# Gated heads in tiles of 128 tokens: three states a head instead of seven, and the output product, norm and rounding one block sooner

## The reference

```python
b = jnp.cumsum(chunks(log_a, dk), axis=2)
b_last = b[:, :, -1:]
q_dec = q * jnp.exp(b)
k_intra = k * jnp.exp(-b)
k_state = k * jnp.exp(b_last - b)

causal = jnp.tril(jnp.ones((C, C), dtype=bool))
scores = jnp.einsum('bnchk,bnshk->bnhcs', q_dec, k_intra)
scores = jnp.where(causal, scores, 0.0)
o_intra = jnp.einsum('bnhcs,bnshv->bnchv', scores, v)

def step(state, inp):
    q_c, k_c, v_c, decay = inp
    o_c = jnp.einsum('bchk,bhkv->bchv', q_c, state)
    state = state * jnp.exp(decay)[..., None] + jnp.einsum('bchk,bchv->bhkv', k_c, v_c)
    return state, o_c
...
o = rmsnorm(o, norm_g).reshape(B, T, D_MODEL)
o = o * jax.nn.silu((r + b_r).astype(f32))
return o.astype(h.dtype) @ w_o
```

## Time and profile before

| | |
|---|---|
| median of 3 runs | 1520.91 us (1520.56 to 1521.14) |
| span of the profiled execution | 1519.9 us |
| TensorE (PE) busy | 1500.9 us, 99% of the span |
| DVE, ACT, POOL busy | 991.4, 658.3, 172.3 us |
| DMA | 182.04 MB, mean 120 GB/s |

### The profile page before, as it was taken

One profiled execution on the slowest core, in us unless ns is written; L12 is line 12 of the kernel. 1 busy time (PEld: TensorE's weight loads), 2 busy tenths in 40 slices (PEclk: granted clock), 3 DMA queues, 4 the chain that ended last, 5 costly groups with the idle time before them and its releaser, 6 DMA issues.

```text
span 1519.9 us, 18779 instructions
## 1 busy us (share of the span) xinstructions
PE 1500.9 (99%) x7424; PEld 1231.2 (81%) x7424; DVE 991.4 (65%) x1620; ACT 658.3 (43%) x1125; POOL 172.3 (11%) x180
## 2 busy tenths in 40 slices
PE   9999999999999999999999999999999999999998
PEld 7788878888888888877777978888888976778786
DVE  7677667966666664877776743434344549989774
ACT  4554444513233233555565532413233446556660
POOL 0000001000000002111111100000000103676200
PEclk9999999999999999999999999999999999999999
DMA  9435444566656653122212343333333231212131
GB/s 374 143 113 166 140 138 149 186 215 183 202 186 201 185 160 107 47 79 70 70 56 84 97 123 92 98 100 94 100 95 99 76 96 61 70 56 72 41 111 56
DMA packets 52840, 182.04 MB, mean 120 GB/s; under 512 B 5984, under 2 KB 7008, under 8 KB 52752
## 3 DMA queue, kind: packets, MB, share of 16 engines
q1 hardware_dynamic: 52752, 180.83, 37.8%
HBM read 177.27 MB, written 3.41 MB: 119 GB/s over the span
## 4 chain that ended last, share of the span: by engine, by line
PE 89%; DVE 6%; ACT 2%; POOL 2%; issue 1%; DVEq 0%; ACTq 0%
PE PS L544 23%; PE PS L547 23%; PE PS L545 23%; PE PS L610 2%; PE PS L824 1%; PE PS L843 1%; PE PS L557 1%; PE PS L554 1%; PE PS L555 1%; POOL sb_TMD L2536 1%; PE PS L1134 1%; PE PS L1140 1%; PE PS L1135 1%; PE PS L629 1%; DVE sb_Wl L1780 1%
## 5 line engine op out<-in xcount | busy, mean ns | idle before, releaser
L544 PE MATMUL PS<-sb_Hh,sb_Wh 128*128 128x512 f32 x1000 | 399.4, 399 | 0.2 <-ACT sb_rg L1376 0.2
L547 PE MATMUL PS<-sb_Hh,sb_Wl 128*128 128x512 f32 x1000 | 390.9, 391 | 0.6 <-DVE sb_Wl L1780 0.6
L545 PE MATMUL PS<-sb_Hl,sb_Wh 128*128 128x512 f32 x1000 | 390.6, 391 | 0.0
L1187 ACT ACTIVATE sb_Wh<-sb_RAW 128x1024 fp32r<-128x1024 f32 x217 | 228.2, 1052 | 287.4 <-PE PS L547 280.7
L1780 DVE TENSOR_TENSOR sb_Wl<-sb_RAW,sb_Wh 128x1024 fp32r<-128x1024 f32 x217 | 268.5, 1238 | 69.6 <-ACT sb_Wh L1187 69.6
L544 PE MATMUL PS<-sb_Oh,sb_Wh 128*128 128x512 f32 x600 | 235.2, 392 | 0.4 <-ACT sb_rg L1376 0.4
L547 PE MATMUL PS<-sb_Oh,sb_Wl 128*128 128x512 f32 x600 | 233.7, 389 | 0.0
L545 PE MATMUL PS<-sb_Ol,sb_Wh 128*128 128x512 f32 x600 | 233.5, 389 | 0.0
L544 PEld LDWEIGHTS PS<-sb_Hh,sb_Wh 128*128 128x128 f32 x1000 | 188.1, 188 | 52.1 <-issue 13.2
L547 PEld LDWEIGHTS PS<-sb_Hh,sb_Wl 128*128 128x128 f32 x1000 | 188.0, 188 | 41.7 <-DVE sb_Wl L1780 1.3
L545 PEld LDWEIGHTS PS<-sb_Hl,sb_Wh 128*128 128x128 f32 x1000 | 188.2, 188 | 39.1 <-issue 1.2
(11 more groups left out here) (433 smaller groups left out, 2061.4 us busy)
## 6 DMA issues: line engine op xcount, KB each, us to landing
sb_RAW<-w SPq DMA_DIRECT2D x128, 512.0 KB, 3.6
sb_ARW<-ada SPq DMA_DIRECT2D x86, 512.0 KB, 4.4
sb_RAW<-diff_in SPq DMA_DIRECT2D x24, 512.0 KB, 3.6
sb_RAW<-gla_in SPq DMA_DIRECT2D x20, 512.0 KB, 3.7
sb_RAW<-in_b SPq DMA_DIRECT2D x16, 512.0 KB, 3.8
sb_RAW<-gla_wo SPq DMA_DIRECT2D x8, 512.0 KB, 3.7
sb_RAW<-diff_wo SPq DMA_DIRECT2D x8, 512.0 KB, 3.5
sb_RAW<-wo SPq DMA_DIRECT2D x8, 512.0 KB, 3.6
```

The source lines that it names most:

```text
L544: mm(to[0:m, :], WH[si][:, k, 0:m], hi[:, k, :], start=first, stop=False)
L545: mm(to[0:m, :], WH[si][:, k, 0:m], lo[:, k, :], start=False, stop=False)
L547: ins = mm(to[0:m, :], WL[si][:, k, 0:m], hi[:, k, :], start=False, stop=last)
L1187: act(WH[slot_of(b)][:, :, 0:m], RAWS[raw_of(b)][:, 0:8 * m].rearrange("p (k m) -> p k m", k=8), ACT.Copy).then_inc(*done("w_hi", b))
```

## The change

Scores, states and outputs are worked out in four tiles of 128 tokens (two chunks) instead of eight chunks, with three states between them.

- **Scores.** The mask `tri` becomes causal over 128 tokens. The key side of `ki` holds only for the same chunk, so `gla_scores` adds, behind the four products of a head, four more of 64x64 that overwrite the corner "second chunk's queries with first chunk's keys", from the new buffer `KS` (decayed keys; its slot 0 is the first chunk of a tile, slot 2 the second, slot 1 the first one times the second's decay, for the state).
- **States.** `KS` takes the place of the buffer `kst` in the ring TD. DVE adds one product of 128x192 into slot 1 (signal `g_ks2`) and a tile's decay `tdec` of 128x4; transposes go from four to three; the increments are three products of all 128 rows and 256 columns; the recurrence has three instructions.
- **Output.** DVE adds one product of 128x192 that gives the first state's decay to the second chunk's queries (third slot of `qd`, signal `g_qo`). `gla_out` has one product of 128 columns with a state for each tile but the first, whose operand is slots 0 and 2 of `qd`.
- **Steps.** "head" has three steps: 1 scores and all states, 2 output, 3 norm and rounding. Head 0 has them at ticks 9 to 11, head 1 at 11 to 13, head 2 at 17 to 19, head 3 at 23 to 25. "r" stands before "head" in the table, and DVE no longer sorts its list.

```diff
-    GLA_TASKS += [(_first[3], "head", _h, 4)] + ([(_first[4], "gates", _h + 1, 1)] if 0 < _h < 3 else [])
     GLA_TASKS += [(_first[5], "r", (_h, 0), 1), (_first[6], "r", (_h, 1), 1)]
+    GLA_TASKS += [(_first[3], "head", _h, 3)] + ([(_first[4], "gates", _h + 1, 1)] if 0 < _h < 3 else [])
...
-                    ins = mm(to[:, ts], ki[:, b, ts], qd[:, b, ts], start=True, stop=True)
+                    mm(to[:, ts], ki[:, b, ts], qd[:, b, t, 0:2].rearrange("p s c -> p (s c)"), start=True, stop=True)
+                e.wait_ge(at("g_kst", h))
+                for t in range(4):
+                    ins = mm(to[0:64, t * 128 + 64:(t + 1) * 128], KS[:, t, 0], qd[:, b, t, 1], start=True, stop=True)
                 ins.then_inc(*done("g_sc", h))
...
+                for t in range(3):
+                    if t != 1:
+                        e.wait_ge(*free[t // 2])
+                    ins = mm(to[t // 2][:, t % 2 * 256:t % 2 * 256 + 256], four(ksT[:, b, :])[:, t, :], gvT[:, b, t, :],
+                             start=True, stop=True)
...
-                e.wait_ge(at("g_sct", h), at("g_state", h, 6))
+                e.wait_ge(at("g_sct", h), at("g_state", h, 2), at("g_qo", h))
...
-                        mm(to, gvT[:, b, t, vs], sct[:, b, t * 128:(t + 1) * 128], start=True, stop=False)
-                        for n in (2 * t, 2 * t + 1):
-                            if n > 0:
-                                u = 64 * (n % 2)
-                                ins = mm(to[:, u:u + 64], GS[:, n - 1, vs], qd[:, b, n * 64:(n + 1) * 64],
-                                         start=False, stop=n % 2 == 1)
+                        mm(to, gvT[:, b, t, vs], sct[:, b, t * 128:(t + 1) * 128], start=True, stop=t == 0)
+                        if t:
+                            ins = mm(to.rearrange("p (s c) -> p s c", c=64), GS[:, t - 1, vs], qd[:, b, t, 0::2],
+                                     start=False, stop=True)
...
+                e.wait_ge(at("g_dec", h))
+                tt(tdec[:, h, :], gdec[:, h, :, 0], gdec[:, h, :, 1], ALU.mult).then_inc(*done("g_tdec", h))
...
-                for kind, a, step in sorted(due(GLA_TASKS, n), key=lambda task: (task[0], task[2]) != ("head", 2)):
+                for kind, a, step in due(GLA_TASKS, n):
...
+                    e.wait_ge(at("g_kst", h), at("g_dec", h))
+                    tt(KS[:, 0:3, 1], KS[:, 0:3, 0], gdec[:, h, 0:3, 1:2].to_broadcast([P, 3, 64]),
+                       ALU.mult).then_inc(*done("g_ks2", h))
...
+                    e.wait_ge(at("evac_d", b), at("g_dec", h))
+                    tt(qd[:, h % 2, 1:4, 2], qd[:, h % 2, 1:4, 1], gdec[:, h, 1:4, 0:1].to_broadcast([P, 3, 64]),
+                       ALU.mult).then_inc(*done("g_qo", h))
...
-    put("tri", (s // 64 == t // 64) & (s <= t))
+    put("tri", s <= t)
```

More of the change, by code:

```diff
@@ L315, in build @@
         flat = lambda x: x.rearrange("p a t -> p (a t)")
-        RAWS = [RAW[:, n, :] for n in range(3)] + [flat(x[:]) for x in (qd, ki, ksT, sct)]
+        RAWS = [RAW[:, n, :] for n in range(3)] + [qd[:].rearrange("p a t s c -> p (a t s c)")[:, 0:1024]] + [flat(x[:]) for x in (ki, ksT, sct)]
         AW = [ARW[:, n, :] for n in range(3)] + [flat(x) for n in range(2) for x in (gvT[:, n], rg[:, n])]
@@ L748, in gla_tick @@
                         to, free = TB.take(("gk", a), ("g_ks", a))
-                        e.wait_ge(at("g_kst", a), *free)
-                        turned(to, TD.buf(("kst", a))).then_inc(*done("g_kt", a))
+                        e.wait_ge(at("g_ks2", a), *free)
+                        for t in range(3):
+                            ins = e.op.transpose(to[:, t * 128:(t + 1) * 128], KS[:, t, 1:3].rearrange("p s c -> p (s c)"),
+                                                 ident)
+                        ins.then_inc(*done("g_kt", a))
                     elif kind == "head" and step == 1:
                         gla_scores(a)
-                        gla_states(a, 0)
+                        gla_states(a)
                     elif kind == "head" and step == 2:
-                        gla_states(a, 4)
-                    elif kind == "head" and step == 3:
                         gla_out(a)
@@ L1357, in gla_tick @@
                         silu_inverse(GLA + 6 * a[0] + 4 + a[1], ("r",) + a)
-                    elif kind == "head" and step == 3:
+                    elif kind == "head" and step == 2:
                         for v in range(2):
@@ L1362, in gla_tick @@
                             act(to, PS[:, 6 + v, :], ACT.Square).then_inc(*done("g_sq", a, v))
-                    elif kind == "head" and step == 4:
+                    elif kind == "head" and step == 3:
                         rows_rstd(("g", a), TA.buf(("gs", a, 0)), 256, "g_rs", a)
@@ L1964, in gates_then, with gla_states @@
                 e.wait_ge(at("g_eb", h))
[L1965 to L1971, removed]
+                e.op.tensor_copy(gdec[:, h].rearrange("p t n -> p (t n)"), chunks(EX[:, h % 2, 0, :])[:, :, 63]).then_inc(*done("g_dec", h))
+                e.wait_ge(at("g_dec", h))
+                tt(tdec[:, h, :], gdec[:, h, :, 0], gdec[:, h, :, 1], ALU.mult).then_inc(*done("g_tdec", h))
+            def gla_states(h):
+                for t in range(3):
+                    src = G45.buf(("gst", h, t // 2))[:, t % 2 * 256:t % 2 * 256 + 256]
+                    e.wait_ge(at("g_kv", h, t // 2))
+                    if t == 0:
                         if h:
@@ L1999, in gla_tick @@
                         tt(four(sct[:, a % 2, :]), four(TB.buf(("gsc", a))), tri, ALU.mult).then_inc(*done("g_sct", a))
[L2000 to L2003, removed]
+                        gla_states(a)
+                    elif kind == "head" and step == 2 and a == 3:
                         s1 = TA.buf(("gs", 3, 0))
```

38 lines of the change are left out of this document (17 added, 21 removed).

## The result

The changed kernel took 1513.12 us (median of 4, 1512.36 to 1516.57) against 1520.74 us of the kernel before on the same chip (1520.55 to 1521.14): a ratio of 0.9949 [0.9936, 0.9962]. In a second measurement it took 1512.89 us (5 runs) against 1521.29, 0.9946 [0.9933, 0.9958]. The profiled execution spans 1511.1 us, 8.8 less than that of before. The forecast was 1511.3 (1510.0 to 1515.0). A line of before stands two or three lines further down now (L736 was L733, L738 L737, L631 L629).

The account below looks back on a forecast made before the run. The prediction took TensorE (PE), busy for 99% of the span, as the bound. Its terms, -7.0 - 4.1 - 0.4 - 0.4 + 2.0 + 0.3 = -9.6 us, gave span 1510.3 and median 1511.3, range 1510.0 to 1515.0.

Parts of the forecast that it names:

- first rival: Scores' narrow products act as another array shape, costing 1.2 us a head instead of 0.5: 1513.9 us, chance 0.14.
- output product: PE, each head: 28 instructions instead of 44 at 0.110 us, saving 1.75 us a head, 7.0 in all.
- increments, with the scores' late end: PE's state products: three of 128 rows replace seven of 64, 2.3 to 1.3 us a head, saving 4.1.
- transposes: PE, each head: one transpose of 0.11 us less, saving 0.4 us in all.
- opening of the output projection: PE's 0.39 us idle for ACT's eviction of block 24 is covered by the output product, saving 0.4 us.
- narrow products: PE, scores: four added 64x64 products, taken as 0.5 us a head, 2.0 in all (1.6 to 4.8).
- stall at head 1's sum, and the rest: PE waits at head 1's sum over rows behind tick 11's chain: 0.3 us added (0 to 1.5).
- pace of 0.11 us an instruction: PE's output product: loading 128 weight columns sets the pace, so 64- and 128-column products cost nearly the same.
- The prediction's own test: Eight narrow instructions between fourth score and first increment take 0.45 us; 0.9 or more speaks for the first rival.
- chain at tick 11: Head 0's norm precedes head 1's states on DVE: third state at t + 9.0 to 9.1, PE wants it t + 9.1.
- collision rival: Tick 11: PE waits for head 1's third state and again its sum, 2 to 3 us: 1513.8, chance 0.11.
- Nothing later takes it back: After the gated stage the saving stays, since PE is busy for 99% of the whole span.

Follow-up runs that it names:

- no_corner: Changed kernel without its four narrow 64x64 products per head and with the mask of before (output not the reference's): 1509.28 us, ratio 0.9921 to the kernel before.
- interleaved: Changed kernel with each narrow 64x64 product directly behind its tile's wide scores product, four visits a head: 1516.74 us, ratio 0.9975 to the kernel before.
- states_late: Changed kernel's arithmetic with all four steps of the kernel before (increments at step 2, output 3, sum 4): 1513.76 us, ratio 0.9953 to the kernel before.
- corner_wide: Changed kernel with 128 weight columns instead of 64 in its four narrow products a head (output not the reference's): 1514.35 us, ratio 0.9959 to the kernel before.
- corner_96: Changed kernel with 96 weight columns instead of 64 in its four narrow products a head (output not the reference's): 1514.52 us, ratio 0.9959 to the kernel before.
- after: The changed kernel itself, in its first measurement and profile: 1513.12 us, ratio 0.9949 to the kernel before.
- corner_48: Changed kernel with 48 weight columns instead of 64 in its four narrow products a head (output not the reference's): 1511.87 us, ratio 0.9942 to the kernel before.
- after_again: The changed kernel once more, nothing altered, to check repeatability: 1512.89 us, ratio 0.9946 to the kernel before.
- both: Changed kernel with the last head's sum over rows one k-step later and head 1's first gate task behind its squares on ACT: 1511.97 us, ratio 0.9942.

## Why the prediction was right

The time fell into the range, 1.8 us above the forecast, and the cause was the one named. The 1.8 us are 0.4 in the stage, 0.4 lost behind it, and 1.0 more between span and median than was allowed. By the time alone this is no proof: 1513.12 lies outside the forecast's own narrower range (1510.2 to 1512.6) and nearer to the first rival's 1513.9 than to 1511.3. It is the timeline that tells them apart. By the prediction's own steps, in us for four heads, start to start in the timelines:

| step | predicted | measured |
|---|---|---|
| output product | -7.0 | -7.0 (19.35 to 12.38) |
| increments, with the scores' late end | -4.1 | -4.3 (12.49, without the 0.39 below, to 8.19 in no_corner) |
| transposes | -0.4 | -0.5 |
| opening of the output projection | -0.4 | -0.4 |
| narrow products | +2.0 | +3.2 |
| stall at head 1's sum, and the rest | +0.3 | -0.2 (what is left of the 9.17) |
| sum | -9.6 | -9.2 |

- The pace of 0.11 us an instruction, whatever the width, held, and operands in two pieces of 64 columns didn't slow it.
- The increments' saving came out as summed, though their old cost was 8 steps of 0.216 us a head and not 7.
- The one step that was off is the price of the narrow products. "I take 0.5, since at 24 us products of 48 and of 128 columns alternate" was the wrong row to lean on: those products stream 512 columns, these 64. Measured is 0.81, halfway to the 1.2 of the first rival, whose mechanism, a shape with a fixed cost per visit, was there at 0.33 us. The other half of the estimate held: its pace of 0.055 for an instruction with 64 weight columns came out at 0.058. The prediction's own test (0.45 against 0.9 between the fourth score and the first increment) showed 0.61 and hid half of the visit, which lies in the neighbours' times. The error of 1.2 was offset by 0.3 in the increments and transposes and 0.5 in the stall and the rest; that the sum was off by 0.4 only is in part luck. The range's high end has a slip too: by its own sum of -5.6 it is 1515.3 and not 1515.0, which changes nothing here.
- The stall at head 1's sum was 0.1, 0.2 with the slower start behind it, in place of 0.3, for the reason given: dear narrow products make PE later. Where they are dearer still (interleaved) it is gone. The chain at tick 11 fitted; DVE's two states that follow the copy, in the changed kernel:

```profile
108.81 1.06 DVE L1981 SCALAR_TENSOR_TENSOR sb_S<-sb_S,sb_tdec,PS 128x256 f32<-128x256 f32 x2
```

  Head 1's third state was done at 109.87, t + 8.8 with t at 101.10, and PE wanted it at 110.44, t + 9.3: 0.6 of reserve in place of none. Without the narrow products (no_corner) both waits of the collision rival appeared, 0.3 each.
- The step saved was costed at 0.4 (the opening); states_late gives 0.34. That the same opening could have cost 1.45 with the increments alone moved ahead, I hadn't seen.
- "Nothing later takes it back" was nearly true: 9.2 at 1228 us, 8.8 at the end, by the late transfer and the waits of the index stage. "The median lies 1.0 above the span" rested on quiet runs: the medians came 1.8 and 2.0 above the profiled span of 1511.1, of which 1.3 is the distance between time and span of the same execution (1512.36 and 1511.1), and the rest fits stretches at the lower clock in the other runs.

## What to carry to other kernels

When TensorE goes through small float32 products, count instructions: one product of 128 streamed columns costs what one of 64 costs, 0.22 us for its pair of instructions. Products of 64 rows on the two halves of the array are the exception: before, they ran side by side in pairs. A product with 64 or 48 weight columns and few streamed ones, among full ones, pays 0.33 us per visit, so gather such products into one visit, and compare with leaving them full: here four narrow ones are 0.08 us a head cheaper than full ones (3.00 against 3.08 in corner_wide). When work moves ahead in a static order, ask at each place that it leaves what wait it had covered there: three increments covered 1.3 us (1.45 to 0.15).

## What the runs showed of the hardware

- Within a row of products of 64 streamed columns, the distance between two instructions is 0.112 us at 128 weight columns (corner_wide), 0.085 at 96 (corner_96), 0.058 at 64 (after) and 0.056 at 48 (corner_48): it falls with the weight columns down to 64 and hardly below. One of 128 streamed and 128 weight columns takes 0.112 as well.
- The visit cost appears with 48 and 64 weight columns and not with 96: 0.33 us, 0.1 of it ahead of the first narrow product, 0.1 within the increments behind, and the rest in the row of narrow products and at its end.
- Products of 64 rows and 256 streamed columns, some for the lower and some for the upper half of the rows, start in pairs 0.01 us apart, with 0.22 us from pair to pair (before, from 84.06), as far as one on all 128 rows stands from the next.
- Stretches at the granted clock's lower level differ from run to run of the same kernel: one more of them made PE 1.3 us later (after_again against after), and slower runs show a lower mean clock (in `both` 0.999 at 1507.50 us, 0.994 at 1516.34).
